# Weight parts requested through GpSimd's DMA queue instead of SyncE's, in a two-layer hybrid decoder on one core

## The reference, cut to what matters

```python
D_MODEL, SEQ, DEPTH = 1024, 512, 2          # D_IN = 2560, D_FF = 2816, float32 throughout
def reference(x, ...):
    for l in range(DEPTH):
        h = rms_norm(x, attn_pre_g[l])
        u = jnp.einsum('bsd,de->bse', h, w_in[l])
        ...                                  # u is split into ten groups of 256 columns
        y_a = conv_mixer(u_conv, ...)        # GLU, causal depthwise conv of 31 taps, LayerNorm, swish
        y_b = retention(rq, rk, rv, rg, ...) # chunks of 128, rotary, GroupNorm, gate
        y_c = moba_attention(mq, mk, mv)     # causal attention, 4 heads of 64
        y_d = pool_mixer(u_pool, ...)        # windowed means, per-group map
        y = jnp.einsum('bse,ed->bsd', jnp.concatenate([y_a, y_b, y_c, y_d], axis=-1), w_out[l])
        x = x + rms_norm(y, attn_post_g[l])
        h = rms_norm(x, ffn_pre_g[l])
        f = jax.nn.silu(h @ w_gate[l]) * (h @ w_up[l])
        x = x + rms_norm(f @ w_down[l], ffn_post_g[l])
    return x
```

## Time and profile before

| | |
|---|---|
| median of the runs | 1102.04 us (1100.69, 1102.04, 1102.1) |
| the profiled execution's own time | 1100.66 us |
| its span in the trace | 1098.9 us |
| TensorE busy / DVE / ACT / POOL | 1081.2 us (98%) / 621.1 (57%) / 410.0 (37%) / 5.2 |
| DMA requests of weight parts | 376 of 256 KB, all on SP's queue |
| mean DMA traffic | 100 GB/s |
| granted TensorE clock | 0.998 |

### The profile page before, as it was taken

The page is one execution under the profiler, slowest core; times in us unless marked ns, Lnnn a source line. Parts: engine busy times, 40 slices in busy tenths (PEclk is TensorE's granted clock), DMA queues, the critical chain, the costliest instruction groups (busy, mean ns, idle before and its releaser), DMA issues.

```text
span 1098.9 us, 16669 instructions
## 1 busy us (share of the span) xinstructions
PE 1081.2 (98%) x6662; PEld 656.5 (60%) x6662; DVE 621.1 (57%) x1419; ACT 410.0 (37%) x810; POOL 5.2 (0%) x18
## 2 busy tenths in 40 slices
PE   8999999999999999999999999999999999999997
PEld 5887894695444444444488888748744444444443
DVE  6998998973432433322579889898633433422014
ACT  5636355553332332221244464456532322331000
POOL 1000000000000000000000000000000000000000
PEclk9999999999999999999999999999999999999999
DMA  8513212254324323323023150134623323232001
GB/s 310 172 56 102 92 40 97 96 166 142 115 77 153 109 83 115 114 79 115 1 79 115 40 151 5 43 111 154 183 86 115 116 96 115 91 101 77 1 20 58
DMA packets 58173, 109.64 MB, mean 100 GB/s; under 512 B 7025, under 2 KB 7281, under 8 KB 57969
## 3 DMA queue, kind: packets, MB, share of 16 engines
q1 hardware_dynamic: 58096, 108.58, 30.8%
HBM read 106.46 MB, written 2.10 MB: 99 GB/s over the span
## 4 chain that ended last, share of the span: by engine, by line
PE 91%; DMA 3%; DVE 3%; ACT 1%; SPq 1%; issue 1%; ACTq 0%; DVEq 0%
PE ps L508 84%; DMA raw<-weights_dram 3%; PE ps L512 3%; PE ps L716 1%; PE ps L700 1%; DVE ring L1158 1%; DMA xs<-x_dram 1%; DVE E L1287 1%; ACT ring L786 0%; PE ps L635 0%; SPq L453 0%; ACT gbc L786 0%; PE ps L677 0%; PE ps L638 0%; PE ps L620 0%
## 5 line engine op out<-in xcount | busy, mean ns | idle before, releaser
L508 PE MATMUL ps<-hT,ring 128*128 128x512 f16 (+1 forms) x3264 | 547.4, 329 | 0.0
L508 PEld LDWEIGHTS ps<-hT,ring 128*128 128x128 f16 x3264 | 319.1, 98 | 221.4
L508 PE MATMUL ps<-ring,U 128*128 128x512 f16 x1440 | 313.4, 379 | 0.0
L1158 DVE SCALAR_TENSOR_TENSOR ring<-raw,ring 128x512 f16<-128x512 f32 x368 | 231.2, 685 | 89.4 <-ACT ring L786 88.7
L786 ACT ACTIVATE ring<-raw 128x512 f16<-128x512 f32 x368 | 208.1, 621 | 126.6 <-PE ps L508 80.4
L508 PEld LDWEIGHTS ps<-ring,U 128*128 128x128 f16 x1440 | 140.8, 98 | 167.2 <-issue 0.3
L1490 DVE SCALAR_TENSOR_TENSOR R<-ps,R 128x512 f32<-128x512 f32 (+1 forms) x52 | 31.7, 609 | 256.2 <-ACT R L961 255.9
L508 PE MATMUL ps<-ring,hT 128*128 128x256 f16 x1152 | 133.3, 273 | 1.4 <-DVE hT L1247 1.3
L961 ACT ACTIVATE R<-ps 128x512 f32<-128x512 f32 (+1 forms) x52 | 27.6, 530 | 276.1 <-PE ps L508 276.0
L508 PEld LDWEIGHTS ps<-ring,hT 128*128 128x128 f16 x1152 | 112.1, 98 | 16.1 <-issue 1.9
L1287 DVE SCALAR_TENSOR_TENSOR E<-E,par 128x256 f32<-128x256 f32 x240 | 102.1, 479 | 0.2
(11 more groups left out here) (109 smaller groups left out, 498.9 us busy)
## 6 DMA issues: line engine op xcount, KB each, us to landing
raw<-weights_dram SPq DMA_DIRECT2D x368, 256.0 KB, 3.3
gbc<-gains_dram SPq DMA_DIRECT2D x8, 512.0 KB, 6.2
xs<-x_dram SPq DMA_DIRECT2D x4, 512.0 KB, 7.0
U<-weights_dram SPq DMA_DIRECT2D x8, 256.0 KB, 7.9
out_dram<-xs SPq DMA_DIRECT2D x8, 256.0 KB, 2.0
cst<-consts_dram SPq DMA_DIRECT2D x1, 1296.0 KB, 12.2
bd<-pool_w_dram SPq DMA_DIRECT2D x8, 16.0 KB, 9.8
par<-params_dram SPq DMA_DIRECT2D x1, 76.0 KB, 6.7
```

The source lines that it names most:

```text
L508: ins = mm(dst, st, mv_, start=first and i == 0, stop=last and i == 2, **kw)
L1158: V.scalar_tensor_tensor(out=ring[:, slot % RING, 1, raw_part(part)], in0=raw_home(n)[0], scalar=W_SCALE, in1=ring[:, slot % RING, 0, raw_ ...
```

## The change

The loop over the parts is cut. SP requests the parts of slots 0 to 2 (n < 12) as before, then the constants and maps, then the gains with their waits alone, one behind the other, and the outputs. The 364 parts from slot 3 on are requested by GpSimd, in a loop behind its scaling of the parameters, with the same waits on `lo_split`. Slot 0 gets semaphores of its own, so that no semaphore is raised from both queues. Buffers, sizes, the order of the parts and the programs of ACT, DVE and TensorE are unchanged.

```diff
-        early_in = [sem(f"early_in{i}") for i in range(EARLY)]
+        early_in = [sem(f"early_in{i}") for i in range(PARTS + EARLY)]
...
-            if PARTS <= n < PARTS + EARLY:
-                e = n - PARTS
-                return ycat_w[:, raw_part(e)], early_in[e], 16
-            m = n if n < PARTS else n - EARLY
+            if n < PARTS:
+                return raw[:, n, :], early_in[n], 16
+            if n < PARTS + EARLY:
+                return ycat_w[:, raw_part(n - PARTS)], early_in[n], 16
+            m = n - PARTS - EARLY
             return raw[:, m % NRAW, :], raw_in[m % NRAW], 16 * (m // NRAW + 1)
...
-            for n in range(PARTS * L * SLOTS):
-                l, at = n // (PARTS * SLOTS), n % (PARTS * SLOTS)
+            for n in range(PARTS + EARLY):
                 if n == PARTS:
                     sp.dma_start(par[:, :, :], params).then_inc(params_in, 16)
                 dst, landed, _ = raw_home(n)
-                if n >= PARTS + EARLY + NRAW:
-                    sp.wait_ge(lo_split, n - NRAW + 1)
-                elif n >= PARTS + EARLY:
-                    sp.wait_ge(lo_split, n - EARLY - NRAW + 1)
                 sp.dma_start(dst, weights[n, :, :]).then_inc(landed, 16)
...
-                if at == PARTS * (GU0 + 3) - 1:
-                    sp.wait_ge(mPT_ps, ths(l, NT - 1, NH - 1))
-                    gain_load(0, l)
-                    sp.wait_ge(mPV, ths(l, NT - 1, NH - 1))
-                    gain_load(3, l)
-                if at == PARTS * (GU0 + 20) - 1:
-                    sp.wait_ge(x_upd, yno("post", l, NT - 1) + 1)
-                    gain_load(2, l)
-                    if l + 1 < L:
-                        sp.wait_ge(xn_sb, xno("fpre", l, NT - 1) + 1)
-                        gain_load(1, l + 1)
+            for l in range(L):
+                sp.wait_ge(mPT_ps, ths(l, NT - 1, NH - 1))
+                gain_load(0, l)
+                sp.wait_ge(mPV, ths(l, NT - 1, NH - 1))
+                gain_load(3, l)
+                sp.wait_ge(x_upd, yno("post", l, NT - 1) + 1)
+                gain_load(2, l)
+                if l + 1 < L:
+                    sp.wait_ge(xn_sb, xno("fpre", l, NT - 1) + 1)
+                    gain_load(1, l + 1)
...
         @block.gpsimd
         def _(pool):
...
+            for n in range(PARTS + EARLY, PARTS * L * SLOTS):
+                dst, landed, _ = raw_home(n)
+                pool.wait_ge(lo_split, n - NRAW + 1 if n >= PARTS + EARLY + NRAW else n - EARLY - NRAW + 1)
+                pool.dma_start(dst, weights[n, :, :]).then_inc(landed, 16)
```

More of the change, by code:

```diff
@@ L446, in _ @@
                         sp.dma_start(xs[:, t, :], x[tok(t), :]).then_inc(x_in[t], 16)
[L447 to L453, removed]
-                if at == PARTS * (GU0 + 3) - 1:
-                    sp.wait_ge(mPT_ps, ths(l, NT - 1, NH - 1))
-                    gain_load(0, l)
-                    sp.wait_ge(mPV, ths(l, NT - 1, NH - 1))
-                    gain_load(3, l)
-                if at == PARTS * (GU0 + 20) - 1:
-                    sp.wait_ge(x_upd, yno("post", l, NT - 1) + 1)
-                    gain_load(2, l)
-                    if l + 1 < L:
-                        sp.wait_ge(xn_sb, xno("fpre", l, NT - 1) + 1)
-                        gain_load(1, l + 1)
+            sp.dma_start(cst[:, P:], consts[:, P:]).then_inc(consts_in, 16)
+            sp.wait_ge(dve_tick, 1)
+            for i in range(L):
+                for g in range(4):
+                    r = slice(HD * (g % 2), HD * (g % 2) + HD)
+                    sp.dma_start(bd[r, i, g // 2, r], pool_w[i, g, :, :]).then_inc(maps_in, 16)
+            for l in range(L):
[8 more added lines that the diff above has]
+                    gain_load(1, l + 1)
             for i in range(2 * NT):
```

## The result

The changed kernel takes 1104.99 us as the median of 6 runs (1103.74 to 1107.72); the kernel before took 1101.46 in the 6 runs beside them (1100.29 to 1102.1). The ratio is 1.0038, 95% interval 1.0024 to 1.0052. It is slower, as forecast, but by 3.5 us (4.2 by the ratio) where 11 were forecast. The profiled execution took 1107.72 us, with a span of 1105.9.

What follows compares the result with a forecast made beforehand. It took landings that hold ACT, and the copies small products need, as what bounds the mixers. Terms 3 + 2 + 1.6 + 2 + 0.6 + 2.0 gave 11.2 us on 1100.7, 1111.9, plus 1.4 for the median: 1113, range 1102 to 1128.

Steps and rivals of the forecast that it cites:

- What bounds: Whole kernel: TensorE busy 98%; weights never late for products, but landings hold ACT and the copies small products need.
- e = 1.0: Every part requested by GpSimd: us added from free buffer to landing against SP; bounds 0.2 and 2.8.
- its 0.4 and a sum of 3.6: Alternative from the skill's first-byte latencies: 0.4 us added per landing, 3.6 us in all instead of 11.2, time 1105.7.
- Start, 0: Slot 3's first parts: requested 1.1 us later plus e, but waiting for bytes anyway; 0 taken, up to 2 us.
- Input projection, +3e + 2e: Layer 0: three chained landings at 36 to 57 us and two at 102 to 111 each add e; 3 + 2 us.
- Where the layers meet, and into gate and up, +1.6, +0.6, +2.0: Landings delay ACT's copies beyond their room: between layers 3e - 1.4, into gate and up of layer 0 and layer 1.
- its term for the gains: Into gate and up: gains requested earlier share the DMA engines with slot 20's parts; 1.7 us in each layer.
- Mixers of layer 1, +2e: One chained landing at 639 us and the next slot's burst each add e; 2 us.
- Requests of 1.0 us queue up ... I let these cancel.: Bursts of four buffers: third request starts 0.8 us later, but spaced landings save 1.0; net taken as nothing.
- Nothing changes: Rival, whole kernel: small e or room at small products keeps time within 0.2%, 1102 to 1104; chance 0.14.
- Faster: Rival, mixers and start: own queue and spaced requests land sooner, at most 5 us gained, 1097; chance 0.07.
- Contention of DVE and GpSimd's requests: Rival, mostly mixers: requests wait for DVE's instruction, 21 us, 1123, or DVE is held, 40 us, 1142; chance 0.12.

Runs made afterwards that it cites:

- the first experiment: The changed kernel with SP holding each pair of gains back to its old place; 1105.24 us, ratio 1.0034 to the kernel before.
- the fourth experiment: The changed kernel with one more short GpSimd instruction of 2 columns ahead of every request; 1121.77 us, ratio 1.0186 to the kernel before.
- seventh experiments: The changed kernel with one more short GpSimd instruction ahead of only the first request of each slot; 1114.31 us, ratio 1.0119 to the kernel before.

## Why the prediction was right in sign and wrong in size

- **What bounds.** Right. TensorE's new idle time is at small products in the mixers, behind copies of ACT that waited for a landing. Nothing was added in gate, up and down, nor by SP's freed time.
- **e = 1.0: the step that failed.** "A request has to set up a read and a write of 128 rows each, which I count as two such instructions (2 x 0.5 - 0.33 = 0.7), and 0.3 for whatever software does". A request is one instruction of 0.54 us, and e is 0.54 to 0.64: 0.27 before it begins and 0.27 to 0.37 on the way. The 0.5 that was doubled there is a mean of ten scalings of 0.19 to 1.14 us, all run while DVE was busy (the earlier trace rows show the mean only); with DVE idle such an instruction takes 0.2. A request takes 538 ns as the median with DVE idle (63 of them) and with DVE busy (220), so the one was no measure of the other. With e = 0.55 the forecast's own sum gives 1.65 + 1.1 + 0.25 + 1.1 + 0 + 1.1 = 5.2 us in place of 11.2. That is 6.0 of the 7.7 us between the 11.2 and the 3.5 measured; the rest is in the places below. The Trainium skill's "DMA: Bandwidth & Descriptors" (Latency and other measured facts), about 0.6 us to the first byte against about 1, came close with its 0.4 and a sum of 3.6: the part behind the request agrees (0.27 to 0.37), and the 0.27 ahead of it are not in that figure. That its sum meets the measured 3.5 is luck: e is larger than 0.4, and the terms are too large elsewhere.
- **Start, 0.** Right as far as the trace shows: slot 3's first part is requested at 17.26 us and not at 16.00, and lands at 23.8 and not at 24.4.
- **Input projection, +3e + 2e.** The place was right, the count too high: in the trace without a drop of the clock layer 0 adds 1.5 us, 0.8 of it before slot 4 is first used (at 62 us), where 5 x 0.55 = 2.75 would stand. Why the landings don't all add up isn't shown; ACT may have some room between them.
- **Where the layers meet, and into gate and up, +1.6, +0.6, +2.0.** Zero. The kernel with only the mixers by SyncE has these parts by GpSimd, and loses nothing; and TensorE's delay in the first experiment's profile stays at 1.5 us from 120 to 638. At e = 0.55 the sum had 0.25, 0 and 1.1 there; the 1.1 of layer 1 was wrong, mostly in its term for the gains, which cost nothing where they come.
- **Mixers of layer 1, +2e.** The trace of the first experiment has 1.9 us there against 1.1: the one place that costs more than its term, by about what one execution is uncertain.
- **"Requests of 1.0 us queue up ... I let these cancel."** At 0.54 us there is no queue: four of GpSimd's in a row take 2.35 us, less than DVE's four splits (2.49), as the two rows above show. In the fourth experiment, with up to 1.2 us for the added instruction and the request, they do queue, and it takes 20 us more than the kernel before, where 8 to 10 were expected without a queue; drops of the clock and the uneven time of the added instruction are in these 20 too.
- **The clock** was in no term. It is some 1.3 us of the mean (7 of 16 runs by 3 us), if the two groups of runs are the clock's, and would be why the profiled execution lies 2.7 us above the median.
- **Rivals.** Nothing changes: excluded by the interval. Faster: no. Contention of DVE and GpSimd's requests: the split takes 680 to 694 ns without them and 681 to 694 with them, and a request takes 538 with DVE busy or idle, so none is seen. The Trainium skill's "SBUF — State Buffer" (Who interferes with whom) expects no lock by DVE's instructions of two inputs in SBUF on the writing of descriptors (as an inference of its own), and the trace agrees. The contention that the rival had in mind does exist for another kind of instruction: the scalings added in the fourth and seventh experiments read SBUF, and took longer with DVE busy, up to 1.77 us. The rule of the Trainium skill's "DMA: Bandwidth & Descriptors" (Rules for kernel authors), that spreading requests over engines saves only issue time, holds for the gain, which is nil; that a longer way from free buffer to landing costs something is not in it.

Open: why the clock should have dropped in 7 executions and not in 9 of much the same programs. The link with the idle time is read from where the drops lie and from the runs' clocks; no run tested it by itself. Open too: what an even delay of 0.3 us at each slot would cost, since no run has one, and whether moving ACT's copies of slot 8 behind its copies of U would remove the stall at 60 us, which no run tests.

## What to carry to other kernels

Ask of a prefetch ring not whether the queue that feeds it is idle, but how long a part takes from a free buffer to its landing, and who stands in line behind the engine that waits for it. Where that wait is on the path, one more buffer (3.4 us here with SyncE) is worth about as much as the choice of the queue (3.5 with four buffers, 2.3 with five), and both can be had. Where buffers fall free in bursts, compare the time of a request with the time that the consumer takes for a part: at 0.54 against 0.69 us the requests kept pace, at 1.2 they queued. And keep instructions that read SBUF off the engine that makes the requests, or measure them while DVE is busy.

## What the runs showed of the hardware

- GpSimd starts a DMA request 0.30 us after the semaphore that it waits for, SyncE 0.03; the request then takes 0.54 us of its queue against 0.33; and a part of 256 KB lands 0.27 to 0.37 us later after its start. GpSimd's request takes 0.54 whether DVE is busy or not.
- A part of 128 rows of 2 KB is 144 packets on SyncE's queue (128 of 2 KB) and 80 on GpSimd's (64 of 4 KB).
- A GpSimd scaling of 2 columns that reads SBUF takes 0.18 to 0.21 us with DVE idle and 0.53 as the median while DVE splits parts; it took 0.56 to 0.74 in 66 of 70 bursts of four splits without a gap, and 1.76 in the other four.
- TensorE's clock was at 1.2 GHz for 6.8 us from 113.2 us on, with 1.5 us of idle time in the 5 of 110 to 115, and in the same place of two other kernels, idle for 1.3 and 1.9 of 5, it stayed at 2.4. The times of the changed kernel and the one with late gains fall into two groups 3 us apart, and the slower group has the lower mean clock.
